# A hybrid decoder step on one core: projections in the order keys, values, gate, deeper rings for the heads' loads, another plan for the pages, the norm's operand by tiles

## The reference, cut to what matters

```python
# layer A: RWKV-7 mixing (projections r, k, v, g; recurrence; w_o), residual
h = h + rwkv7_mix(rmsnorm(h, a_norm), ...)
# shared keys and values, from another norm of the same stream
k, v = split(rmsnorm(h, kv_norm) @ w_kv)            # also outputs
# layer B: stick-breaking attention, strictly causal
q, g = split(rmsnorm(h, b_norm) @ w_qg)
z = q . k / sqrt(128) + bias[head]
log_keep = where(mask, log_sigmoid(-z), 0)
log_rest = reverse_cumsum(log_keep) - log_keep
att = where(mask, exp(log_sigmoid(z) + log_rest), 0)
h = h + ((att @ v) * silu(g)) @ w_o
y = rmsnorm(h, final_norm)
```

## Time and profile before

| | |
|---|---|
| median of 3 runs | 2167.6 us |
| profiled execution | 2165.69 us, span 2164.2 us |
| busy | PE 1926.6 us, DVE 979.3, ACT 817.6, POOL 260.7 |
| DMA | 508.82 MB, 235 GB/s over the span |
| mean granted clock of PE | 0.956 of full speed |

### The profile page before, as it was taken

One profiled execution on the slowest core, in us unless ns is written; L12 is line 12 of the kernel. 1 busy time (PEld: TensorE's weight loads), 2 busy tenths in 40 slices (PEclk: granted clock), 3 DMA queues, 4 the chain that ended last, 5 costly groups with the idle time before them and its releaser, 6 DMA issues.

```text
span 2164.2 us, 49253 instructions
## 1 busy us (share of the span) xinstructions
PE 1926.6 (89%) x20796; PEld 1645.9 (76%) x20796; DVE 979.3 (45%) x1520; ACT 817.6 (38%) x1423; POOL 260.7 (12%) x311
## 2 busy tenths in 40 slices
PE   5799999999799999969899989899898897677697
PEld 3599999999688888869899766566666665344497
DVE  6346354544455555523553443533333332367244
ACT  3523232333355555522332444422322332466232
POOL 2200000000244344303100000000000000010032
PEclk8899999999899999989999999999999999799798
DMA  5445555553222222144565999999999999899541
GB/s 190 156 157 163 180 168 172 165 162 123 73 72 72 70 80 67 46 168 151 196 223 176 364 418 419 396 406 418 419 419 413 418 406 395 310 347 389 217 153 68
DMA packets 119493, 508.82 MB, mean 235 GB/s; under 512 B 19233, under 2 KB 60578, under 8 KB 65826
## 3 DMA queue, kind: packets, MB, share of 16 engines
q1 hardware_dynamic: 119298, 506.00, 62.5%
HBM read 472.33 MB, written 33.63 MB: 234 GB/s over the span
## 4 chain that ended last, share of the span: by engine, by line
PE 28%; DMA 21%; DVE 2%; ACT 2%; issue 2%; SPq 1%; DVEq 0%; ACTq 0%
DMA at_vraw<-in_cache_v 21%; PE psP_ L2075 7%; PE psP_ L2076 7%; PE psP_ L2077 7%; PE at_psO L2123 4%; PE at_psS L2101 2%; SPq L1540 1%; DMA at_vS<-o_kv 0%; PE psP_ L2171 0%; ACT at_p_w L1840 0%; ACT at_p_w L1838 0%; PE psP_ L2196 0%; DVEq L1432 0%; DVE wlo_ L1882 0%; DMA wraw_<-in_weights 0%
## 5 line engine op out<-in xcount | busy, mean ns | idle before, releaser
L2075 PE MATMUL psP_<-xhi,whi_ 128*128 128x320 f32 x1536 | 492.3, 321 | 22.0 <-DVE wlo_ L1882 14.1
L2076 PE MATMUL psP_<-xlo,whi_ 128*128 128x320 f32 x1536 | 477.7, 311 | 0.0
L2077 PE MATMUL psP_<-xhi,wlo_ 128*128 128x320 f32 x1536 | 477.5, 311 | 0.0
L2075 PEld LDWEIGHTS psP_<-xhi,whi_ 128*128 128x128 f32 x1536 | 291.9, 190 | 88.9 <-issue 71.1
L134 PE MATMUL psP<-xhi,whi 128*128 128x320 f32 x1024 | 318.2, 311 | 14.6 <-DVE wlo L169 12.9
L1882 DVE TENSOR_TENSOR wlo_<-wraw_,whi_ 128x2048 fp32r<-128x2048 f32 x96 | 222.1, 2314 | 216.4 <-ACT whi_ L1712 215.5
L135 PE MATMUL psP<-xlo,whi 128*128 128x320 f32 x1024 | 317.4, 310 | 0.0
L136 PE MATMUL psP<-xhi,wlo 128*128 128x320 f32 x1024 | 317.4, 310 | 0.0
L1712 ACT ACTIVATE whi_<-wraw_ 128x2048 fp32r<-128x2048 f32 x96 | 183.6, 1913 | 322.7 <-PE psP_ L2077 317.4
L2076 PEld LDWEIGHTS psP_<-xlo,whi_ 128*128 128x128 f32 x1536 | 292.1, 190 | 0.0
L2077 PEld LDWEIGHTS psP_<-xhi,wlo_ 128*128 128x128 f32 x1536 | 291.4, 190 | 0.0
(11 more groups left out here) (313 smaller groups left out, 2667.6 us busy)
## 6 DMA issues: line engine op xcount, KB each, us to landing
at_kraw<-in_cache_k SPq DMA_DIRECT2D x128, 1024.0 KB, 10.8
at_vraw<-in_cache_v SPq DMA_DIRECT2D x128, 1024.0 KB, 11.1
wraw_<-in_weights SPq DMA_DIRECT2D x96, 1024.0 KB, 6.7
wraw<-in_weights SPq DMA_DIRECT2D x64, 1024.0 KB, 4.9
rw_s0t<-in_s0T SPq DMA_DIRECT2D x16, 256.0 KB, 3.5
o_wkv_s<-rw_SN SPq DMA_DIRECT2D x16, 256.0 KB, 2.5
resT<-in_xT SPq DMA_DIRECT2D x4, 640.0 KB, 5.8
spill_r<-stage SPq DMA_DIRECT2D x4, 640.0 KB, 7.4
```

The source lines that it names most:

```text
L2075: pe.matmul(out, wh, c_.xhi[:, kc, :], start=(kc == 0), stop=False)
L2076: pe.matmul(out, wh, c_.xlo[:, kc, :], start=False, stop=False)
L2077: last = pe.matmul(out, wl, c_.xhi[:, kc, :], start=False, stop=(kc == NM - 1))
```

## The change

1. Projections in the order q, keys, values, gate. The operand changes twice: to kv_norm before the keys, back to b_norm before the gate.
2. Plan: a chunk beside blocks 13.4 (was 12.7), a block 12.0 (12.2), heads 4.0 after the last chunk (22.0) and 7.8 each (7.6), a new-token step 12.0 (15.0), `ENDING` 1.8 blocks after the last (2.6).
3. `Q`, `K`, `V` are rings of four (two) and lie, with kN, vS, vnew and late, in the place of `wraw` alone; qn, st_new, er, o_new get places of their own. `G` is a ring of six (four). Head loads start after the last chunk's split; the gate's wait for the groups' stores one by one.
4. bo's chunks 0 and 1 are loaded when the new-token steps are over, 2 and 3 when the last head is scored and its values turned.
5. The first quarter of the operand after wo's norm goes tile by tile through DVE, ACT and DVE, with a semaphore for each tile on which the first bank's matmuls wait; the split of chunk 16 is written behind the norm's sums.
6. The last product with `rs` goes by tiles, 11 on DVE and 5 on POOL, stored as 4, 4, 3 and 5 tiles.

```diff
-PROJ = ["r", "k", "v", "g", "wo", "q", "g2", "kk", "kv", "bo"]
+PROJ = ["r", "k", "v", "g", "wo", "q", "kk", "kv", "g2", "bo"]
-KRING, VRING, GRING = 2, 3, 4
+KRING, VRING, HRING, GRING = 2, 3, 4, 6
-CHUNK, SHARED = 7.0, 12.7
+CHUNK, SHARED = 7.0, 13.4
-BLOCK = 12.2
+BLOCK = 12.0
-HEADS, HEAD = WINDOW + 48 * SHARED + 22.0, 7.6
-NEWS, NEWLY = HEADS + 4.0, 15.0
-ENDING = SAMPLE + BLOCK * (NK + 2.6)
+HEADS, HEAD = WINDOW + 48 * SHARED + 4.0, 7.8
+NEWS, NEWLY = HEADS + 4.0, 12.0
+ENDING = SAMPLE + BLOCK * (NK + 1.8)
...
 def split_time(i):
     first = first_chunk(BO)
     if first <= i < first + 2:
-        return ENDING - 30.0 + 5.0 * (i - first)
+        return head_time(NHB - 1, 2.9) + 2.2 * (i - first)
     return chunk_time(i - 1) + 0.2
+def low_time(i):
+    if i == 16:
+        return evacuation_time(15, 3) + 1.8
+    return split_time(i) + 2.4
 def load_time(i):
     first = first_chunk(BO)
-    return max(split_time(i - 4) + 5.0, ENDING - 50.0 if i >= first else 0.0) + 0.01 * (i % 4)
+    if first <= i < first + 2:
+        return new_time(NB, 0.4) + 0.1 * (i - first)
+    if first + 2 <= i < first + 4:
+        return head_time(NHB - 1, 0.5) + 0.1 * (i - first)
+    return low_time(i - 4) + 2.6 + 0.01 * (i % 4)
...
                 if i == first_chunk(BO):
                     Nv.wait(sp, "gate", NB - 1)
+                elif i == first_chunk(BO) + 2:
                     sp.wait_ge(p_z, NHB)
+                    sp.wait_ge(p_vturned, NHB)
...
             def heads():                     # SyncE
                 for h in range(NHB):
-                    j = h % 2
-                    yield max(head_time(h - 2, 0.3), HEADS - 8.0)
-                    if h == 0:
-                        sp.wait_ge(c_.bank_full, kv_done)
-                        sp.wait_ge(c_.stored, spilled_before(VP))
-                    if h >= 2:
-                        sp.wait_ge(p_scored, h - 1)
+                    j = h % HRING
+                    yield max(head_time(h - HRING, 0.4), low_time(first_chunk(BO) - 1) + 2.7)
+                    if h >= HRING:
+                        sp.wait_ge(p_scored, h - HRING + 1)
+                        sp.wait_ge(p_vturned, h - HRING + 1)
                     sp.dma_start(Q[j][:], c_.spill[SP_I["q"]][h][:, 0:SEQ]).then_inc(p_q_in[j], 16)
                     sp.dma_start(K[j][:], c_.spill[SP_I["kk"]][h][:, 0:SEQ]).then_inc(p_k_in[j], 16)
-                    yield max(head_time(h - 2, 0.5), HEADS - 5.0)
-                    if h == 0:
-                        sp.wait_ge(c_.stored, spilled_before(BO))
-                    if h >= 2:
-                        sp.wait_ge(p_vturned, h - 1)
                     sp.dma_start(V[j][:], c_.spill[SP_I["kv"]][h][:, 0:SEQ]).then_inc(p_v_in[j], 16)
             def gates():
                 for h in range(NHB):
-                    yield max(head_time(h - GRING, 2.5), HEADS - 4.0)
+                    yield max(head_time(h - GRING, 2.3), HEADS + 16.5 if h >= 4 * 3 else HEADS - 1.0)
+                    if h == 0:
+                        sp.wait_ge(c_.bank_full, heads_from)
                     if h >= GRING:
                         sp.wait_ge(p_y, h - GRING + 1)
+                    elif h % 4 == 0:
+                        sp.wait_ge(c_.stored, spilled_before(G2) + 16 * (h // 4 + 1))
                     sp.dma_start(G[h % GRING][:], c_.spill[SP_I["g2"]][h][:, 0:SEQ]).then_inc(p_g_in[h % GRING], 16)
...
             def ending():                    # POOL, before and after
-                y = quarter(c_.resT, 3)
-                pool.tensor_tensor(y, y, rs[:].unsqueeze(1).to_broadcast([P, 4, TOK]), ALU.mult).then_inc(y_ready[3], 1)
+                for m in range(11, NM):
+                    yield ENDING + 16 * CHUNK + 5.0
+                    if m == 11:
+                        pool.wait_ge(c_.rs_ready, 3)
+                        pool.wait_ge(y_scaled, NM)
+                    pool.tensor_tensor(c_.resT[:, m], c_.resT[:, m], rs[:], ALU.mult).then_inc(y_ready, 1)
...
+            def scaled(m, gain):             # DVE
+                v = VEC[gain] * NM + m
+                dve.scalar_tensor_tensor(out=xtmp[:, m % 4], in0=c_.resT[:, m], scalar=c_.vec[:, v:v + 1], in1=rs[:],
+                                         op0=ALU.mult, op1=ALU.mult).then_inc(c_.xtmp_ready, 1)
+            def operands():
+                for m in range(5):
+                    yield chunk_time(16) - 5.5 + 0.6 * m
+                    if m == 0:
+                        dve.wait_ge(c_.rs_ready, 2)
+                    if m < 4:
+                        scaled(m, "b_norm")
+                    if 1 <= m < 4:
+                        dve.wait_ge(first_hi, m)
+                        dve.tensor_tensor(c_.xlo[:, m - 1], xtmp[:, m - 1], c_.xhi[:, m - 1],
+                                          ALU.subtract).then_inc(first_x, 1)
+                    elif m == 4:
+                        dve.wait_ge(c_.xhi_ready, 17)
+                        dve.tensor_tensor(c_.xlo[:, 3], xtmp[:, 3], c_.xhi[:, 3], ALU.subtract).then_inc(c_.x_ready, 1)
+                for j in range(17, 28):
+                    q, before, gain = j % 4, (QP, QP, KP, G2)[j // 4 - 3], "kv_norm" if 20 <= j < 24 else "b_norm"
+                    yield (chunk_time(16 + q) - 6.0 if j < 20 else chunk_time(first_chunk(before) - 3 + q) + 1.0)
...
```

More of the change, by code:

```diff
@@ L1337, in _ @@
             stages(front, products, run)
-WO, QP, G2, KP, VP, BO = (PB[x] for x in ("wo", "q", "g2", "kk", "kv", "bo"))
+WO, QP, KP, VP, G2, BO = (PB[x] for x in ("wo", "q", "kk", "kv", "g2", "bo"))
 GW0 = 4 * WO
@@ L1490, in trunk @@
                         ("v", "z sp rc arg o gate")))
-        p_q_in, p_k_in, p_v_in = ([sem(f"p_{x}_in{j}") for j in range(2)] for x in "qkv")
+        p_q_in, p_k_in, p_v_in = ([sem(f"p_{x}_in{j}") for j in range(HRING)] for x in "qkv")
         p_g_in = [sem(f"p_g_in{j}") for j in range(GRING)]
@@ L1635, in _ @@
             side_by_side(weights(), pages(), stores(), news(), heads(), gates())
-            for q in range(4):
-                sp.wait_ge(y_ready[q], 1)
-                sp.dma_start(quarter(a["o_y"], q), quarter(c_.resT, q)).then_inc(y_stored, 16)
+            for m0, m1 in ((0, 4), (4, 8), (8, 11), (11, NM)):
+                if m1 < NM:
+                    sp.wait_ge(y_normed, m1)
+                else:
+                    sp.wait_ge(y_ready, 5)
+                sp.dma_start(a["o_y"][:, m0:m1], c_.resT[:, m0:m1]).then_inc(y_stored, 16)
             sp.wait_ge(y_stored, 64)
@@ L1714, in gates @@
             def gates():
-                for i in range(first_chunk(G2) + 3, first_chunk(KP), 4):
+                for i in range(first_chunk(G2) + 3, first_chunk(BO), 4):
                     n, grp, q, g_all = parts(i)
@@ L1743, in operands @@
             def operands():
-                for q in range(4):
-                    yield chunk_time(16 + q) - 4.0
-                    act.wait_ge(c_.xtmp_ready, 4 * (16 + q + 1))
-                    act.activation(quarter(c_.xhi, q), xtmp[:], ACT.Copy).then_inc(c_.xhi_ready, 1)
-                for q in range(4):
-                    yield chunk_time(first_chunk(KP) - 3 + q) + 3.6
-                    act.wait_ge(c_.xtmp_ready, 4 * (20 + q + 1))
-                    wait_chunk_used(c_, act, 4 * G2 + 3, q)
+                for j in range(16, 28):
+                    q, before = j % 4, (QP, QP, KP, G2)[j // 4 - 3]
+                    if j == 16:
+                        for m in range(4):
+                            yield chunk_time(16) - 4.5 + 0.6 * m
+                            act.wait_ge(c_.xtmp_ready, 4 * 16 + m + 1)
+                            act.activation(c_.xhi[:, m], xtmp[:, m], ACT.Copy).then_inc(c_.xhi_ready if m == 3 else first_hi, 1)
+                        continue
+                    yield (chunk_time(16 + q) - 4.0 if j < 20 else chunk_time(first_chunk(before) - 3 + q) + 3.6)
+                    act.wait_ge(c_.xtmp_ready, 4 * (j + 1))
+                    if j >= 20:
+                        wait_chunk_used(c_, act, 4 * before - 1, q)
                     act.activation(quarter(c_.xhi, q), xtmp[:], ACT.Copy).then_inc(c_.xhi_ready, 1)
@@ L1914, in norm @@
                     dve.tensor_tensor(acc, acc, sq[1 + m % 2], ALU.add).then_inc(acc_ready, 1)
-            def operand(j, q, gain):
-                if j > 16:
-                    dve.wait_ge(c_.x_ready, j)
-                for m in range(4 * q, 4 * q + 4):
-                    v = VEC[gain] * NM + m
-                    dve.scalar_tensor_tensor(out=xtmp[:, m % 4], in0=c_.resT[:, m], scalar=c_.vec[:, v:v + 1], in1=rs[:],
-                                             op0=ALU.mult, op1=ALU.mult).then_inc(c_.xtmp_ready, 1)
-                dve.wait_ge(c_.xhi_ready, j + 1)
-                dve.tensor_tensor(quarter(c_.xlo, q), xtmp[:], quarter(c_.xhi, q), ALU.subtract).then_inc(c_.x_ready, 1)
@@ new lines, in operands @@
+            def operands():
[15 more added lines that the diff above has]
```

(8 more changed lines are left out.)

78 lines of the change are left out of this document (32 added, 46 removed).

## The result

The changed kernel takes 2175.1 us (median of 20 runs, 2167.1 to 2181.0) beside 2166.3 us (20 runs, 2156.4 to 2173.2) for the kernel before: a ratio of 1.0041, 95% interval 1.0029 to 1.0053. It is 0.4% slower, 9 us, where I forecast 13.6 us faster. Its profiled execution took 2177.7 us, span 2176.0.

The account below looks back on a forecast made before the run. Bytes bound the stretch of chunks beside blocks, while SyncE's one load order kept the tail from being full. Gains 12 + 3.3 + 0.3 less losses 1 and 1 gave 13.6 us: 2165.7 - 13.6 = 2152, range 2136 to 2174.

Parts of the forecast that it names:

- The operand by tiles, and the split behind the norm's sums: Before the query projection: PE starts sooner, 3.3 us gained, plus 0.3 us for the moved split.
- Third change of operand: End of the query projection: the added operand change is just covered; 1 us lost, bounds 0 and 4 x 1.5.
- The first stage: Weight chunks beside sample blocks, bound by bytes: 3.5 more blocks make it 36 us longer, taken out of the tail.
- The switch: From the gate's last chunk to the first head's score: 8 us in place of 34.
- The tail anew: From the last chunk to the heads' and blocks' end: 158 us, with 36 us added before it 194 against 206.
- 8.84 us a head as a price to carry over: Heads' stage: 16 heads at the old kernel's 8.84 us each, within a chain of 159 us.
- "What is late next" at the end: End of the tail: the lonely 31 us of blocks go; first output matmul at 2019 or so.
- Rings: SyncE's queue beside the heads: 40.7 us of waits for scores go; gate's wait nothing, at most 16 x 1 us.
- rival 1: Tail stays as long as before, 206 us at 358 GB/s; only 1.6 us gained: 2164 us; chance 0.25.
- "408 GB/s is not to be had with such loads": Tail: 142 us at 408 GB/s was ruled out with the heads' 128 KB loads running.
- The end: Last product with rs by tiles on DVE and POOL: 9.2 us for 7.9; 1 us lost, bounds -2.5 and +1.5.
- rival 2: New-token steps still take 17.9 us each, leaving heads behind: tail and growth 224 against 206, 2182 us; chance 0.13.

Follow-up runs that it names:

- e4: Kernel before with only the operand after wo's norm by tiles and chunk 16's split behind the norm's sums: 2163.6 us, 0.9980.
- e1: Changed kernel without the load of the samples' gate; DVE writes gS itself, tile by tile: 2165.7 us, 0.9993.
- e9: Changed kernel with the new-token steps planned every 15.0 instead of 12.0: 2165.4 us, 0.9983.
- e3: Changed kernel without the load of gS and with the first two output chunks' splits ahead of the last block's copy: 2160.7 us, 0.9959.
- e5: e3 with the new-token steps planned every 15.0 instead of 12.0: 2153.5 us, 0.9943.
- e6: e3 with rings of two for q, k, v and of four for the gate again: 2159.7 us, 0.9968.
- e7: e3 with the gates' loads one head time later in SyncE's queue: 2162.5 us, 0.9978.
- e10: e5 with the heads' rings back to two and the ending's last product by quarters as in the kernel before: 2150.4 us, 0.9913.
- e8: e3 with the plan constants of the kernel before, heads still 4.0 after the last chunk: 2170.7 us, 1.0025.

## Why the prediction was wrong

Its time, 2152, missed by 23 us, and the result lies just above its range; the sign was wrong. Step by step:

- *The operand by tiles, and the split behind the norm's sums: right.* 3.6 us forecast; 4.3 measured alone.
- *Third change of operand: 1 us forecast, 0.2 measured.* The query projection's 16 chunks end 121.0 us after wo's last, against 125.0 before and 120.8 in e4, which hasn't the third change.
- *The first stage: right in kind, 4 us short.* 632.2 became 672.0, 39.8 more for the forecast's 36. At the end of the last chunk 52 blocks' copies have run instead of 48; four blocks of 4.19 MB at 410 GB/s are 41 us. I counted 3.5.
- *The switch: right.* 8 us forecast, 6.3 measured. Yet I looked for "what is late next" only up to the first score and found the gate's evacuation. The sentence should have been followed for each load that the reordering puts last, and the samples' gate is one. The samples' values were the late load before, 10.2 us; the change hands that role to `gS`, and I had written down only that it leaves the values.
- *The tail anew: this is the step that failed.* Forecast 166.5 in the measure of the table, measured 187.6, 21 over. The prediction priced the tail by its bytes (151 to 162 us) and by the heads' own chain (159), and took nothing new to be late. Neither was the bound: the changed tail moves 315 GB/s. The runs give three causes: the gate's load (13.2 us of tail from the changed kernel to e1, 10 in the times), the new tokens' density (13.9 us of tail from the changed kernel to e9, part of it the load's, and 7.9 from e3 to e5), and the output splits (4.8 or 1.9 us after the last head). They overlap, since a later step hides the load in part. In e5, with the load gone and the steps at 15, the tail is 164.2. That it meets the forecast is partly luck: e5 still has 15.0 us between heads 2 and 3 and 9.1 at the end, which no term had, and it moves 343 GB/s from 1856 to 2012, not 375.
- *8.84 us a head as a price to carry over: wrong under denser steps.* It was measured with steps at 15.0, and I used it for a plan with 12.0. From head 3 to 16 it measured 9.6 there and 8.8 with 15.0 again. Over all heads it was 10.5, beyond the 9.5 that the prediction names as a sign of being wrong.
- *"What is late next" at the end: missing.* I removed the 31 us in which three blocks ran alone and didn't ask what had run in their shade. It was ACT's 3.7 us and DVE's 4.6 us of splits. The first output matmul came at 2044.2, where I had expected 2019.
- *Rings: the waits didn't go.* I had called the 40.7 us an argument against rival 1. With rings of four and six SyncE waits 39.9 us for the gates' product instead, where I had put "nothing, and at most 16 x 1 us"; and e6, with the old depths, is as fast as e3.
- *"408 GB/s is not to be had with such loads": wrong.* e1 moves 408 GB/s from 1863 to 1895 with the heads' loads among the pages. It didn't matter, since bytes were not the bound.
- *The end: right.* 1 us of loss forecast, 0.9 measured (16.8 against 15.9). DVE took 7.8 us for 11 tiles with POOL's 5.3 us beside it (in order of time, then by line in ns min/median/max and starts):

```profile
2162.84 7.82 DVE L2073 TENSOR_TENSOR resT<-resT,at_rs 128x320 f32<-128x320 f32 x11 [1.96 <-ACT at_rs L1753]
2163.41 5.30 POOL L1707 TENSOR_TENSOR resT<-resT,at_rs 128x320 f32<-128x320 f32 x5 [26.00 <-ACT resT L1886]
```

```profile
L2073 DVE TENSOR_TENSOR resT<-resT,at_rs x11: 477/491/1147, 2162.8 to 2170.2; 128x320 f32<-128x320 f32 x11
...
L1707 POOL TENSOR_TENSOR resT<-resT,at_rs x5: 1047/1098/1100, 2163.4 to 2167.6; 128x320 f32<-128x320 f32 x5
```

One by one the two engines take turns: five of DVE's tiles take 1.14 us, the other six 0.48 to 0.49, and POOL's five start 1.05 us apart. That is the exclusion by whole instructions of which the prediction's page of the Trainium skill speaks ("SBUF — State Buffer", "SBUF: two separate sides"), and this trace agrees with it again. The 9.2 us were too many for another reason. They took 3.67 / 4 = 0.92 for a tile of POOL, but POOL's 3.67 us began at 2152.42, while DVE's first product ran until 2153.35: 0.93 us of it were POOL's own wait. Without them a tile is 0.69 us, and 11 x 0.41 + 5 x 0.69 = 8.0, near the 7.8. By the same token the old end was 7.0 us (2151.9 to 2158.8), not 7.9.

Of the rivals, rival 2 came nearest, in time (2182, 7 us off) and in mechanism. In its measure, tail and growth of the first stage together, the kernel before has 206, rival 2 said 224, and the changed kernel has 219, where the forecast said 194. Its step of 17.9 us was measured as 17.5. Its order was right, too: it said that 12.3 heads are done with the last step and the others follow at 8.84; 12 are scored when the last step begins, and the last four follow at 8.75. What it didn't have is what makes the 17.5. It took a step to be that long, but 27.9 us of the first step hold the late load, and without the load a step is 16.0 (e3). With 16.0 its sum gives 8 + 128 + 33 + 4 + 36 = 209 against 206, and e3 has 206. So rival 2's place and bookkeeping hold, and its 224 was reached in part by a load that it didn't know of. What I wrote against it, that the 17.9 us were the length of two heads and not of the steps' chain, failed: with 1.54 heads beside it, 13.6 us at 8.84, a step got 2 us shorter and not 4. Rival 1's tail of 206 was passed by 13 us. The load of `gS`, 10 us, was in no rival.

What stays open: why head 2 to 3 still takes 13 to 15 us in e1, e3, e5, e7 and e10 and 10.0 in e6; how much of the heads' pace is the granted clock; and whether `gS` issued before the value page would have done as well as no load at all, which no run tried.

## What to carry to other kernels

When a step's order is turned, list every small load that now comes last and follow it through its queue: one of 512 KB behind a page's slot cost 10 us. And follow it to the end, since what it stalls can hold the queue again. When a stretch of idle engines is planned away, write down what ran in its shade, since that is on the path afterwards. A pace measured under one plan holds for that plan: planned times only say what lies beside what, and a step planned at 12 still took 16 us, with fewer heads beside it. An instruction that waits has its wait in its duration; take it out before using the duration as a price.

## What the runs showed of the hardware

- A load of 512 KB landed 10.9 us after its issue with page loads in flight before it (`gS`); the 640 KB store of the gate's last tiles took 10.9 us as well.
- PE's granted clock was 0.71 in the old switch (PE busy 15.3 of 35 us), 0.74 in the new hole (16.7 of 32) and 0.71 in e8's last 58 us (26.4 busy). These are means over the two levels: after PE was busy 8.1 of 10 us at 1.00 (1861 to 1871), in the hole it was 0.50 (1.2 GHz) from 1872 to 1881, 1.00 (2.4 GHz) from 1882 to 1888 and 0.50 again from 1889 to 1898. A hole isn't what decides it: in e1 the mean was 0.74 over the same stretch, 1863 to 1895, with PE busy 26.9 of 32 us.
- Four more blocks in a byte-bound stretch cost about their bytes: 39.8 us against 16.8 MB at 410 GB/s, 41 us (36.5 to 42.1 us in the other kernels with 52 blocks there).
- DVE's and POOL's products in the ending (`L2073`, `L1707`) exclude each other for a whole instruction and take turns: 1.05 us for a pair of 128x320 tiles, with DVE's 0.49 us tile shown as 1.14 and POOL's as 1.10.
